# Three unused 32-byte tiles that shift the SBUF addresses of the transposed inputs xT and the hidden tiles hT

## What is computed

```python
def first_block(x, ...):                 # depth 2
    y = (b_gate * conv3(c_gate * h)) @ w_out          # layer 0: [b_gate, c_gate, h] = x @ w_in
    x = layer_norm(ALPHA * x + y)
    x = layer_norm(ALPHA * x + square(relu(x @ w1)) @ w2)     # w1 1024x4096, w2 4096x1024
    y = mla_attention(x) @ w_o                        # layer 1: latent attention, 8 heads
    x = layer_norm(ALPHA * x + y)
    x = layer_norm(ALPHA * x + square(relu(x @ w1)) @ w2)

def second_block(x, c, ...):             # depth 2
    h = modulate(rmsnorm(x), shift, scale)            # shift, scale, gate from silu(c) @ mod_w
    x = x + gate * (rglru(h @ w_in) @ w_out)
    k, v = split(modulate(rmsnorm(x)) @ w_kv)
    x = x + gate * ((attention(q, k, v) * silu(g)) @ w_out)   # [q, g] = h @ w_in
    return rmsnorm(x)
```

## Time and profile before

| | |
|---|---|
| median of 3 runs | 780.79 us (780.48 to 935.18) |
| the profiled execution, first to last instruction (span) | 778.4 us |
| median less span | 2.4 us |
| granted TensorE clock, mean | 0.998 |
| TensorE (PE) busy | 768.9 us, 99% |
| weight loads (PEld) busy | 697.1 us, 90% |
| VectorE (DVE) busy | 586.1 us, 75% |
| ScalarE (ACT) busy | 405.1 us, 52% |

### The profile page before, as it was taken

How to read it: one execution, slowest core, us unless ns; L and a number is a source line. 1 busy time by engine, 2 the same in 40 slices (tenths; PEclk the granted TensorE clock), 3 DMA queues, 4 the chain that set the end, 5 groups by cost and what they waited for, 6 DMA issues and landing times.

```text
span 778.4 us, 12084 instructions
## 1 busy us (share of the span) xinstructions
PE 768.9 (99%) x4982; PEld 697.1 (90%) x4982; DVE 586.1 (75%) x786; ACT 405.1 (52%) x512; POOL 34.6 (4%) x66
## 2 busy tenths in 40 slices
PE   9999999999999999999999999999999999999996
PEld 9999888988998889888889988998799988999995
DVE  5886898868688697687989776676687877756754
ACT  5455235545445424875355444445649869664632
POOL 0000000000000001000000000000500051000001
PEclk9999999999999999999999999999999999999999
DMA  9877438897867731446488977876235254754102
GB/s 351 319 274 278 184 125 324 348 320 289 313 231 288 290 122 62 163 139 267 165 326 344 347 273 275 308 263 245 103 109 216 109 216 163 270 216 164 55 3 80
DMA packets 26983, 173.94 MB, mean 223 GB/s; under 512 B 3248, under 2 KB 3632, under 8 KB 7856
## 3 DMA queue, kind: packets, MB, share of 16 engines
q1 hardware_dynamic: 26640, 173.14, 60.0%
q10 hardware_dynamic: 288, 0.02, 0.0%
HBM read 172.10 MB, written 1.05 MB: 222 GB/s over the span
## 4 chain that ended last, share of the span: by engine, by line
PE 93%; DVE 3%; ACT 2%; POOL 1%; issue 0%; POOLq 0%; ACTq 0%
PE bank L578 12%; PE bank L580 12%; PE bank L579 12%; PE Y L714 10%; PE Y L716 10%; PE Y L713 10%; PE bank L1067 2%; PE bank L1068 2%; PE bank L1069 2%; PE bank L996 2%; DVE w_low L1610 1%; PE bank L816 1%; PE Y L738 1%; PE bank L610 1%; PE bank L619 1%; PE bank L611 1%
## 5 line engine op out<-in xcount | busy, mean ns | idle before, releaser
L1610 DVE TENSOR_TENSOR w_low<-raw,w_high 128x2048 fp32r<-128x2048 f32 (+3 forms) x125 | 278.5, 2238 | 65.1 <-ACT w_high L1203 62.8
L1203 ACT CAST w_high<-raw 128x2048 fp32r<-128x2048 f32 (+3 forms) x125 | 232.5, 1869 | 92.9 <-DMA raw<-weights 80.0
L578 PE MATMUL bank<-xT_h,w_high 128*128 128x256 f32 x728 | 206.5, 284 | 0.1
L579 PE MATMUL bank<-xT_l,w_high 128*128 128x256 f32 x728 | 205.8, 283 | 0.0
L580 PE MATMUL bank<-xT_h,w_low 128*128 128x256 f32 x728 | 205.8, 283 | 0.0
L578 PEld LDWEIGHTS bank<-xT_h,w_high 128*128 128x128 f32 x728 | 139.4, 192 | 1.6 <-DVE w_low L1610 0.3
L579 PEld LDWEIGHTS bank<-xT_l,w_high 128*128 128x128 f32 x728 | 139.4, 191 | 1.1
L580 PEld LDWEIGHTS bank<-xT_h,w_low 128*128 128x128 f32 x728 | 139.5, 192 | 0.0
L714 PE MATMUL Y<-w_low,hT_h 128*128 128x512 f32 x324 | 128.3, 396 | 0.0
L713 PE MATMUL Y<-w_high,hT_h 128*128 128x512 f32 x324 | 128.0, 395 | 0.0
L716 PE MATMUL Y<-w_high,hT_l 128*128 128x512 f32 x324 | 101.9, 395 | 0.0
(11 more groups left out here) (291 smaller groups left out, 1144.5 us busy)
## 6 DMA issues: line engine op xcount, KB each, us to landing
raw<-weights SPq DMA_DIRECT2D x149, 1024.0 KB, 5.0
rows<-rows_in SPq DMA_DIRECT2D x9, 512.0 KB, 7.7
raw<-weights SPq DMA_DIRECT2D x4, 576.0 KB, 3.5
z<-gates_in SPq DMA_DIRECT2D x4, 512.0 KB, 3.8
raw<-weights SPq DMA_DIRECT2D x2, 896.0 KB, 4.4
raw<-weights SPq DMA_DIRECT2D x3, 512.0 KB, 7.0
x<-x_in SPq DMA_DIRECT2D x2, 512.0 KB, 4.4
kT<-rows_in SPq DMA_DIRECT2D x2, 512.0 KB, 8.3
```

The source lines that it names most:

```text
L578: mm(dst, high, xh[:, kt, :], start=kt == 0, stop=False)
L579: mm(dst, high, xl[:, kt, :], start=False, stop=False)
L1203: nc.scalar.copy(w_high[:, n % RING, start:COLS[n]], raw[:, s % RAW, start:COLS[n]]).then_inc(w_high_ready, 1)
L1610: tt(w_low[:, n % RING, start:COLS[n]], slot[:, start:COLS[n]], f32(w_high[:, n % RING, start:COLS[n]]), ALU.subtract).then_inc(raw_done, 1)
```

## The change

Three tiles of 8 fp32 columns (32 bytes) that nothing reads or writes are allocated between the others:

```diff
         x = sb("x", [P, TB, D])
         z = sb("z", [P, TB, D])
+        sb("space_1", [P, 8])
         xT_h = sb("xT_h", [P, KT, SEQ], F32R)
         xT_l = sb("xT_l", [P, KT, SEQ], F32R)
+        sb("space_2", [P, 8])
         stage = sb("stage", [P, 2, 512])
...
         cols = sb("cols", [P, NCOL])
+        sb("space_0", [P, 8])
         modcol = sb("modcol", [P, 2 * NMOD])
```

## The result

| | before | after |
|---|---|---|
| median | 780.64 us (4 runs) | 770.15 us (4 runs, 769.35 to 770.40) |
| span of the profiled execution | 778.4 us | 768.6 us |
| PE busy | 768.9 us | 757.9 us |
| PEld busy | 697.1 us | 689.4 us |
| DVE, ACT busy | 586.1, 405.1 us | 586.4, 405.1 us |

The ratio is 0.9867, with a 95% interval from 0.9854 to 0.9881. The forecast was 774.2 us with a range from 771.2 to 780.9; the time lies 1 us beneath the range. A difference of less than 2% is called "same" here, but the interval is clear of 1. (One run of the kernel before took 935.18 us; the ratio leaves it out.)

A forecast was written before the change was run, and what follows sets the result against it. TensorE, busy 99%, was taken to bound the kernel, so matmul steps add up: -6.6 - 4.6 + 0.9 + 4.2 - 0.5 = -6.6 us, from 780.8 to 774.2 us. The range was 771.2 to 780.9 us.

The forecast's parts named there:

- term 6: Other moved tiles, used by VectorE, ScalarE and GpSimd, and plain fp32 products: no effect, as those engines have time free.
- Term 1: hT stationary, now at a multiple of 64: 996 matmuls go from 233.3 to 226.7 ns, 6.6 us less.
- Term 2: xT moving, now off a multiple of 64: 2304 matmuls at 2.0 ns less each, 4.6 us less.
- term 3: hT moving, now at a multiple of 64: 444 matmuls at 2.0 ns more each, 0.9 us more.
- wide part of term 4: xT stationary, now off a multiple of 64, 512 columns: 336 matmuls at 6.7 ns more each, 2.3 us more.
- rival B: Nothing changes, as hT's cost could hang on its address, writer or reading time: 780.8 us, chance 13%.
- rival C: Slower: a moving operand off its multiple costs as much as a stationary one: 793.3 us; with anything else slower, 6%.
- Term 4, narrow: xT stationary, now off a multiple of 64, 448 or 256 columns: 288 matmuls at 6.7 ns, 1.9 us more.
- rival D: Narrow products with the stationary tile off gain too, since what counts is that the two differ: 771.7 us, chance 12%.
- term 5: Part of the added xT stationary cost runs into TensorE's waits for ScalarE and VectorE: 0.5 us less.

The follow-up runs named there:

- e1: Against the kernel before, only hT moved, to a multiple of 64 bytes (192 from the weights by 256): 775.14 us, ratio 0.9931.
- e3: Against the kernel before, weights, xT and hT all 32 bytes off a multiple of 64 (distances xT 0, hT 192): 775.37 us, ratio 0.9936.
- e12: Changed kernel's distances kept (xT 32, hT 0), but weights shifted 32 bytes, so xT and hT have the kernel before's remainders by 64: 769.67 us.
- e5: Against the kernel before, xT placed 64 bytes and hT 0 behind the weights, by 256: 772.12 us, ratio 0.9891.
- e11: Against the kernel before, xT placed 208 bytes (a 16-byte step) and hT 0 behind the weights, by 256: 773.81 us, ratio 0.9919.
- e6: Against the kernel before, xT and hT both placed 192 bytes behind the weights, by 256: 763.94 us, ratio 0.9787.
- e9: Against the kernel before, xT placed 192 bytes and hT 0 behind the weights, by 256: 767.75 us, ratio 0.9835.

## Why the prediction was right where it was, and what failed

**Right.** What bounds the kernel: TensorE in one unbroken row, so that what a matmul saves, the span saves; the sum of the steps' differences is the whole 9.8 us. Every other engine was idle enough (term 6). The plain fp32 products didn't react: the gates (L996) have 215.9 ns before and 215.8 after. The signs of terms 1, 2, 3 and of the wide part of term 4 were right, and rival B, "nothing changes", and rival C, slower, are refuted by the result. The argument for B was the 16-byte line of the Trainium skill, page "SBUF — State Buffer", section "Specifications (TRN2)"; every address tried lies at the start of such a line, and they differ by up to 6 ns per matmul. The page's line size alone doesn't give the cost of an operand here.

**The premise failed:** "I take it that the differences above come from the remainder by 64". They come from the distance to the weights, which counts by 256 bytes and in steps finer than 32 (e1, e3, e12, e5, e11): e1 and e3, with all remainders different and all distances equal, took 775.14 and 775.37 us. In the kernel before the weights were at a multiple of 64 in every pairing, so the trace couldn't tell a tile's own remainder from its distance; nor did I ask whether 160, 32 and 96 would be the same, all "32 off". From this follow the two terms that were mis-sized:

- **Term 4, narrow.** "I take 6.7, as the same operand is the one that is off: 1.9 us more." Measured: 1.2 ns less with 256 columns, 0.5 more with 448, 0.1 us less in all. This is 2.0 us of the miss. The role of the operand decides nothing for a narrow product, its offset does: these went from offset 0 to 224. The lower end of the bounds, and rival D at 12%, had it.
- **Term 2.** 2304 x 2.0 = 4.6; measured 6.7. hT's 117.8 ns in the earlier trace rows belong to an offset of 160, and xT went to 32, which has 117.0 in the mean and 116.7 in long rows: 2.7 to 3.3 ns less than before. This is 2.1 us of the miss. The bound of 2.2 ns that I had given as the best case was none: it was the price of another offset.
- **Term 1** was too large by 1.3 us. 6.7 ns is the difference in long rows of "down"; in the changed kernel the first of a "down" behind an "up" piece have steps of up to 236 ns, and the mean difference is 5.7.
- **The wide part of term 4 and term 5** together: forecast 1.8, measured 1.1. The step rose by 5.4 ns, not 6.7, which is 342 x 5.4 = 1.8 us; 0.7 of it fell into waits, close to the 0.5 of term 5.
- **hT moving (term 3)** cost 0.7 more instead of 0.9, and the start 0.5 us more. The start's part is 1.4 us of waiting for the first input, less 0.9 because the granted clock rose earlier (at 4.0 us and not at 6.7). The wait isn't the change's own mark: the traces of nine other placements have it with 0.2 to 1.4 us, three have none.

These are the 3.2 us by which the span was missed (771.8 forecast, 768.6 measured). The time was missed by 0.8 us more, since the forecast put 2.4 us around the span, the median of three runs less the span of another execution. Every execution on record has 1.8 or 1.9 us around its own span, and the median after is 1.6 over the profiled span.

Where a forecast was met, it was in part luck. Rows with hT at 160 moving were taken for rows with xT at 32, and the sign came out the same. The feed-forward of layer 1 became 3.9 us shorter, as the 3.8 forecast, but by 1.8 in "down" instead of 2.6 and 1.8 in "up" instead of 1.2; the two errors cancel. Two readings in the rivals were wrong, without weight for the outcome: rival C begins at 2.0 / 2304 = 0.9 ns, not at 0.4, and in B the difference of 1.38 to 1.40 us is half of that to rows 4, not a third.

Of the rivals' ideas D's was the true one, that the two operands' difference counts, but its argument for wide products, that they are dear when the two differ, holds for most offsets only: at 64 they cost 229.

## What to carry to other kernels

In this kernel, where TensorE runs without a pause, the place of two tiles relative to each other in SBUF was worth 0 to 2% at no cost in work: spacers of 32 bytes gave 1.3%, another placement (xT and hT 192 bytes behind the weights by 256) 2.1%, and a third (96 and 128) nothing. Read the cost as the step from start to start over long rows of one form, and treat a pairing that isn't in the trace as unknown, even if it looks like one that is. Measure the offset itself in steps of 32 bytes and finer; a rule like "a multiple of 64" drawn from one program holds only as long as the other operand stays where it is.

## What the runs showed that was not expected

- The step of a float32r matmul of 128x128 with 256 columns varied between 113.3 and 120.0 ns with the offset (and, at 192, with the pace), that of one with 512 columns between 226.7 and 234 ns, at the same granted clock (0.997 to 0.999). Plain fp32 products had 216 ns at offsets of 160 and of 0.
- A row of one form can hold two steady paces in the same kernel, 117.8 and 113.3 ns (e6, e9), with the same operands, and keeps to one for tens of microseconds. What ran ahead of it seems to take part, but two kernels with the same addresses and the same matmuls up to there took different paces at 12 us, so neither placement nor the order of the work settles it.
- What in the chip makes the cost is open. That the load of the next stationary tile and the stream of the moving one, both read from SBUF at once, hinder each other would fit a cost by difference; no run here took one of the two away, so this is a guess.
